# Layer two's first feed-forward: the input projection by seven block products in place of eight

## The reference, cut to what matters

```python
def ada_norm(x, g, shift, scale):
    return rms_norm(x, g) * (1.0 + scale) + shift
def swiglu(h, w_in, w_out):
    a, b = jnp.split(h @ w_in, 2, axis=-1)
    return (jax.nn.silu(a) * b) @ w_out
...
x = x + 0.5 * mx[:, 2] * swiglu(ada_norm(x, norm_g[l, 0], mx[:, 0], mx[:, 1]), ffn_w_in[l, 0], ffn_w_out[l, 0])
hctx = hctx + 0.5 * mc[2] * swiglu(ada_norm(hctx, norm_g[l, 0], mc[0], mc[1]), ffn_w_in[l, 0], ffn_w_out[l, 0])
```

## Time and profile before

| | |
|---|---|
| Median of 3 runs | 2319.11 us (2318.86 to 2327.45) |
| Profiled execution, first to last instruction (span) | 2314.2 us |
| The profiled execution's own time | not listed apart from its span; the two are compared in the prediction |
| Mean granted TensorE clock | 0.987 of full speed |
| TensorE (matmul) | busy 2227.1 us, 96% of the span, 19320 matmuls |
| VectorE | 1145.4 us, 49% |
| ScalarE | 846.8 us, 37% |
| GpSimd | 176.3 us, 8% |
| DMA | 315.76 MB, 136 GB/s on the mean |

### The profile page before, as it was taken

How to read it: one execution, slowest core, us unless ns; L and a number is a source line. 1 busy time by engine, 2 the same in 40 slices (tenths; PEclk the granted TensorE clock), 3 DMA queues, 4 the chain that set the end, 5 groups by cost and what they waited for, 6 DMA issues and landing times. The chain is left out here.

```text
span 2314.2 us, 46991 instructions
## 1 busy us (share of the span) xinstructions
PE 2227.1 (96%) x19320; PEld 2091.2 (90%) x19320; DVE 1145.4 (49%) x1930; ACT 846.8 (37%) x1384; POOL 176.3 (8%) x150
## 2 busy tenths in 40 slices
PE   6999999899999999998999999999999999999998
PEld 5986798799999999976999999999999998979998
DVE  5227375653433445456653333454343446487665
ACT  4226454632221233248432222243232234455444
POOL 0003112100000010501200000010000010001000
PEclk9999999999999999999999999999999999999999
DMA  9853544445676244520354666242233233225573
GB/s 297 234 167 86 172 133 104 128 147 154 186 216 186 86 131 117 149 80 28 102 175 141 190 207 189 84 126 85 81 114 94 86 96 101 74 82 146 168 202 112
DMA packets 515900, 315.76 MB, mean 136 GB/s; under 512 B 16035, under 2 KB 513274, under 8 KB 515622
## 3 DMA queue, kind: packets, MB, share of 16 engines
q1 hardware_dynamic: 515160, 313.45, 46.1%
q10 hardware_dynamic: 590, 0.16, 0.0%
HBM read 312.50 MB, written 1.06 MB: 135 GB/s over the span
## 5 line engine op out<-in xcount | busy, mean ns | idle before, releaser
L1118 PE MATMUL ps<-h_hi,w_hi 128*128 128x256 f32 x3376 | 728.0, 280 | 3.5 <-DVE h_lo L1726 1.7
L1118 PE MATMUL ps<-h_lo,w_hi 128*128 128x256 f32 x3376 | 720.6, 278 | 0.0
L1118 PE MATMUL ps<-h_hi,w_lo 128*128 128x256 f32 x3376 | 720.6, 278 | 0.0
L1118 PEld LDWEIGHTS ps<-h_hi,w_hi 128*128 128x128 f32 x3376 | 537.8, 189 | 22.9 <-issue 21.6
L1118 PEld LDWEIGHTS ps<-h_lo,w_hi 128*128 128x128 f32 x3376 | 539.4, 189 | 0.1
L1118 PEld LDWEIGHTS ps<-h_hi,w_lo 128*128 128x128 f32 x3376 | 537.9, 189 | 0.0
L1960 DVE TENSOR_TENSOR w_lo<-stage,w_hi 128x1024 fp32r<-128x1024 f32 x227 | 285.0, 1258 | 441.5 <-ACT w_hi L1467 440.9
L1467 ACT ACTIVATE w_hi<-stage 128x1024 fp32r<-128x1024 f32 x227 | 236.6, 1055 | 334.4 <-PE ps L1118 200.4
L1960 DVE TENSOR_TENSOR w_lo<-deep,w_hi 128x1024 fp32r<-128x1024 f32 x184 | 226.1, 1234 | 226.9 <-ACT w_hi L1467 225.2
L1467 ACT ACTIVATE w_hi<-deep 128x1024 fp32r<-128x1024 f32 x184 | 191.9, 1055 | 179.7 <-PE ps L1118 141.4
L1118 PE MATMUL ps<-g_hi,w_hi 128*128 128x256 f32 x1100 | 232.9, 280 | 0.2
(11 more groups left out here) (413 smaller groups left out, 2858.0 us busy)
## 6 DMA issues: line engine op xcount, KB each, us to landing
modw<-in_ada_w SPq DMA_DIRECT2D x72, 1024.0 KB, 6.7
stage<-in_ffn_w_in SPq DMA_DIRECT2D x88, 512.0 KB, 3.9
deep<-in_ffn_w_in SPq DMA_DIRECT2D x88, 512.0 KB, 3.9
modw<-in_w_mod SPq DMA_DIRECT2D x18, 1024.0 KB, 6.1
stage<-in_w_in SPq DMA_DIRECT2D x30, 512.0 KB, 5.3
stage<-in_ffn_w_out SPq DMA_DIRECT2D x32, 384.0 KB, 3.5
stage<-in_even_w_in SPq DMA_DIRECT2D x24, 512.0 KB, 4.0
deep<-in_ffn_w_out SPq DMA_DIRECT2D x32, 384.0 KB, 3.4
```

The source lines that it names most:

```text
L1118: last = mm(ps[:, j, v - a:v - a + SEQ], w_part[wp][:, u % RING, c, :], x_part[xp][:, x, v:v + SEQ], start=first and wp == xp and v == a, ...
```

## The change

The product of tokens and a pair of units is seen as a product of 2x2 blocks. The tokens are cut into quarters: 256 latent or context tokens by the first or last 4 chunks of 128 input rows. The weights of a pair are cut likewise: gate unit or up unit by the first or last 4 chunks. Eight block products (of 12 matmuls of 128x256 each) become seven, with sums of blocks as operands, and sums of the results.

- *Weight halves.* Of each pair, seven halves of 128x512 are split into high and low parts: B11 and B21 (the gate unit's), B22 (the up unit's second), and four sums T1 = B12 − B11, T3 = B22 − B12, T2 = T3 + B11, T4 = B21 − T2. GpSimd forms the sums (`pool_seven`), two of them in place over the fetched unit, T1 and T4 in buffers of their own (`t1_raw`, `t4_raw`). ScalarE makes the high part of each half (`act_half`), VectorE the low one (`dve_half`). The ring of 4 units becomes a ring of 8 halves.
- *Token sums.* The seam leaves the tokens in `h_hi` and `h_lo`. GpSimd adds the two for four quarters (`x_quarter`, 128x1024 each) and forms two of the four sums, VectorE the other two; each of the four is split by ScalarE and VectorE.
- *Products.* TensorE goes through the seven in the order of `seven_order`, the next pair's B11, B21, B22, T2 and T1 woven with T3 and T4 of the one before. B11, T3, T4 and T2 add up in one bank (X1, two in turn), the others go to Y1, W1 and Z1.
- *Results.* ScalarE copies three of the results out of PSUM (128x256: `keep_p1`, `keep_z`, `keep_u3`), VectorE adds (`c11`, `u2`, `c12`, `c22`, with one operand in PSUM), ScalarE applies silu to latent and context gate apart (`gate`), GpSimd multiplies gate and up (`gated`, 128x512), ScalarE and VectorE make the high and low part (`high`, `low`).
- *Where.* The second half does all 11 pairs so; the first half does one pair as before (`conv=1`) and 8 in the new way. The seam runs 2 units ahead instead of 3 (`lead=2`). The first half's down projection no longer splits the first units of the next phase; its last block makes the high and low parts of B11 and B21 instead (`opens`). SP fetches a gate unit into its slot only after T4 and T2 of the pair that had it.
- Some tiles (`cst`, `convt`, `wgate`, parts of `vtok`, `big`, `stage`) lend their space, and new counters share semaphores with counters of the mixers (`SHARED`).

```diff
+def seven_order(w):
+
+    order = [("B11", 0)]
+    for p in range(-1, w):
+        here = [("T3", p)] + [("B21", p + 1), ("B22", p + 1)] + [("T4", p)] + [("T2", p + 1), ("T1", p + 1)] + [("B11", p + 2)]
+        order += [(kind, n) for kind, n in here if 0 <= n < w]
+    return order
...
+        def seam(tail, start, norm, dst=None, segs=0, latent=False, lead=LEAD):
+        def seven(w, col0, n, dst, conv=0, sums=False, turn=0):
+
+            units = 2 * (conv + n)
+            r = {"unit_done": units, "w_hi": units + LEAD - 2 * conv, "w_ready": units + LEAD - 2 * conv, "prod": 6 * n, "e_hi": 5 * n, "e_ready": 5 * n,
+                 "t_sum": 4 * n, "c11_sum": n, "u2_sum": n, "c22_sum": n, "c12_sum": n, "p1_kept": n, "z_kept": n, "u3_kept": n, "a_lat": n, "a_ctx": n, "gt_ready": n,
+                 "g_hi_ready": conv + n, "g_ready": conv + n, "bank_free0": conv, "bank_free1": conv}
+            if sums:
+                r.update({"f_full": 4, "s_sum": 2, "s_diff": 2, "sum_hi": 4, "sum_ready": 4})
+            add("seven", r, w=w, col0=col0, n=n, dst=dst, conv=conv, sums=sums, turn=turn, order=seven_order(n))
...
+                if fast:
+                    seven(w, (0, FH)[half] * P + (2 - 2 * half) * P, (FH - 3, FH)[half], (3, 0)[half], conv=1 - half, sums=half == 0, turn=2 * half)
...
+                         fed=not (last and i and half) and not (fast and not half), peel=i and half, opens=fast and not half, hper=hpers[2 * half + 1], **w_down)
...
+            seam(tail, ("ffn_w_in_2", 1, 0), (1, 0), lead=2)
...
+        def half_slot(p, kind, n):
+
+            return (place(p, kind, n) + 2 * (first_unit(p) + p.kw["turn"])) % (2 * RING)
...
+        def raw_half(p, kind, n):
+
+            b, a = (arrival(first_unit(p) + 2 * n + i)[0] for i in range(2))
+            return {"B11": a[:, 0:4, :], "B21": a[:, 4:8, :], "B22": b[:, 4:8, :], "T2": a[:, 0:4, :], "T3": b[:, 0:4, :],
+                    "T1": t1_raw[:, :, :], "T4": t4_raw[:, :, :]}[kind]
...
+            for n in range(k["n"]):
+                col = k["col0"] + (k["conv"] + n) * P
+                eng.wait_ge(S("w_ready"), u0 + 2 * n - DEEP + 1)
+                fetch(u0 + 2 * n, col + D_FF)
+                if n < 2:
+                    eng.wait_ge(S("w_ready"), u0 + 2 * n + 1 - DEEP + 1)
+                else:
+                    eng.wait_ge(S("t_sum"), p.at("t_sum", 4 * (n - 2) + 4))
+                    eng.wait_ge(*half_signal(p, "lo", "T2", n - 2))
+                fetch(u0 + 2 * n + 1, col)
...
+            def product(kind, n, bank, tokens, first):
+                eng.wait_ge(*half_signal(p, "lo", kind, n))
+                at = half_slot(p, kind, n)
+                for c in range(KC // 2):
+                    for wp, xp in W_X:
+                        last = mm(ps[:, bank, 0:SEQ], half[wp][:, at, c, :], tokens(xp, c), start=first and c == 0 and wp == xp,
+                                  stop=c == KC // 2 - 1 and wp == "lo", skip_group_check=True)
+                up(last, "unit_done", by=2) if kind == "T4" else up(last, "prod")
...
+            p1(0)
+            for n in range(-1, w):
+                here, ahead = X1[n % 2], X1[(n + 1) % 2]
+                if n >= 0:
+                    eng.wait_ge(S("u2_sum"), p.at("u2_sum", n + 1))
+                    summed(n, 4)
+                    product("T3", n, here, sum_of(3), False)
+                if n + 1 < w:
+                    eng.wait_ge(S("c11_sum"), p.at("c11_sum", n + 1))
+                    product("B21", n + 1, W1, tokens_of(1, 0), True)
+                    eng.wait_ge(S("z_kept"), p.at("z_kept", n + 1))
+                    summed(n + 1, 2)
+                    product("B22", n + 1, Z1, sum_of(4), True)
+                if n >= 0:
+                    eng.wait_ge(S("u3_kept"), p.at("u3_kept", n + 1))
+                    product("T4", n, here, tokens_of(1, 1), False)
+                if n + 1 < w:
+                    eng.wait_ge(S("p1_kept"), p.at("p1_kept", n + 2))
+                    product("T2", n + 1, ahead, sum_of(2), False)
+                    summed(n + 1, 3)
+                    eng.wait_ge(S("c22_sum"), p.at("c22_sum", n + 1))
+                    eng.wait_ge(S("c12_sum"), p.at("c12_sum", n + 1))
+                    product("T1", n + 1, Y1, sum_of(1), True)
+                if n + 2 < w:
+                    p1(n + 2)
...
+            for n in range(-1, w):
+                act_half(eng, p, "T1", n + 1)
+                if n == w - 1:
+                    act_after_halves(eng, p, 0)
+                if n + 1 < w:
+                    keep_p1(n + 1)
+                if n >= 1:
+                    high(n - 1)
+                if n >= 0:
+                    keep_u3(n)
+                act_half(eng, p, "B11", n + 2)
+                act_half(eng, p, "T3", n + 1)
+                if n + 1 < w:
+                    gate(n + 1, 0)
+                    keep_z(n + 1)
+                act_half(eng, p, "B21", n + 2)
+                act_half(eng, p, "B22", n + 2)
+                if n >= 0:
+                    gate(n, 1)
+                act_half(eng, p, "T4", n + 1)
+                act_half(eng, p, "T2", n + 2)
+            act_after_halves(eng, p, 1)
+            high(w - 1)
+            act_after_halves(eng, p, 2)
 
...
+                    if k.get("opens") and i * step + j == k["n"] - 1:
+                        dve_half(eng, phases[phases.index(p) + 1], "B11", 0)
+                        dve_half(eng, phases[phases.index(p) + 1], "B21", 0)
...
+            if k["sums"]:
+                eng.wait_ge(S("f_full"), p.at("f_full", 3))
+                up(V.tensor_tensor(x_sum[2], x_quarter[2], x_quarter[0], ALU.subtract), "s_diff")
+                dve_half(eng, p, "B11", 0)
+                dve_half(eng, p, "B21", 0)
+                eng.wait_ge(S("f_full"), p.at("f_full", 4))
+                eng.wait_ge(S("s_sum"), p.at("s_sum", 2))
+                up(V.tensor_tensor(x_sum[3], x_quarter[3], x_sum[1], ALU.subtract), "s_diff")
...
+            for n in range(-1, w):
+                dve_half(eng, p, "T1", n + 1)
+                if n >= 0:
+                    c12(n)
+                    c22(n)
+                dve_half(eng, p, "B11", n + 2)
+                if n == w - 1:
+                    dve_split(eng, u0 + 2 * w)
+                if n >= 1:
+                    low(n - 1)
+                if n + 1 < w:
+                    c11(n + 1)
+                for kind, ahead in (("T3", 1), ("B21", 2), ("B22", 2)):
+                    dve_half(eng, p, kind, n + ahead)
+                if n + 1 < w:
+                    u2(n + 1)
+                dve_half(eng, p, "T4", n + 1)
+                dve_half(eng, p, "T2", n + 2)
+            dve_split(eng, u0 + 2 * w + 1)
+            low(w - 1)
+            dve_split(eng, u0 + 2 * w + 2)
...
+            def sums(n):
+                (b, full_b, arrived_b, _), (a, full_a, arrived_a, _) = (arrival(u0 + 2 * n + i) for i in range(2))
+                eng.wait_ge(full_b, arrived_b)
+                eng.wait_ge(full_a, arrived_a)
+                if n:
+                    eng.wait_ge(*half_signal(p, "lo", "T1", n - 1))
+                up(G.tensor_tensor(t1_raw[:, :, :], b[:, 0:4, :], a[:, 0:4, :], ALU.subtract), "t_sum")
+                eng.wait_ge(S("t_sum"), p.at("t_sum", 4 * n + 1))
+                up(G.tensor_tensor(b[:, 0:4, :], b[:, 4:8, :], b[:, 0:4, :], ALU.subtract), "t_sum")
+                eng.wait_ge(S("t_sum"), p.at("t_sum", 4 * n + 2))
+                eng.wait_ge(*half_signal(p, "lo", "B11", n))
+                up(G.tensor_tensor(a[:, 0:4, :], b[:, 0:4, :], a[:, 0:4, :], ALU.add), "t_sum")
+
+            def last_sum(n):
+                a = arrival(u0 + 2 * n + 1)[0]
+                eng.wait_ge(S("t_sum"), p.at("t_sum", 4 * n + 3))
+                if n:
+                    eng.wait_ge(*half_signal(p, "lo", "T4", n - 1))
+                up(G.tensor_tensor(t4_raw[:, :, :], a[:, 4:8, :], a[:, 0:4, :], ALU.subtract), "t_sum")
+
+            def gated(n):
+                for name in ("a_lat", "a_ctx", "c12_sum", "c22_sum"):
+                    eng.wait_ge(S(name), p.at(name, n + 1))
+                eng.wait_ge(S("g_ready"), p.at("g_ready", k["conv"] + n))
+                up(G.tensor_tensor(gt[:, :], gate_of[n % 2], plain, ALU.mult), "gt_ready")
+
+            if k["sums"]:
+                eng.wait_ge(S("w_ready"), p.at("unit_done") - 4)
+                for chunks, v, i, ready in ((0, 0, 2, 4), (1, 0, 3, 8), (0, 1, 0, 12), (1, 1, 1, 16)):
+                    eng.wait_ge(S("h_ready"), p.at("h_ready", ready - 2 * KC))
+                    up(G.tensor_tensor(x_quarter[i], quarter(h_hi, chunks, v).bitcast(F32), quarter(h_lo, chunks, v).bitcast(F32), ALU.add), "f_full")
+                eng.wait_ge(S("f_full"), p.at("f_full", 4))
+                up(G.tensor_tensor(x_sum[0], x_quarter[0], x_quarter[1], ALU.add), "s_sum")
+                eng.wait_ge(S("s_sum"), p.at("s_sum", 1))
```

(37 more changed lines are left out.)

211 lines of the change are left out of this document (192 added, 19 removed).

## The result

The changed kernel takes 2323.61 us (median of 20 runs), the kernel before beside it 2318.99, a difference of 4.6 us between the medians. The ratio estimated from all the runs is 1.0024, 95% interval 1.0013 to 1.0034, or 5.6 us slower (3.0 to 7.9). The forecast was 2321, within 0.5%. 228 matmuls fewer (19 × 12) bought nothing. The profiled execution has a span of 2319.7 us, 5.5 above that of before.

What follows compares the result with a forecast made beforehand. VectorE and GpSimd alternating, 10.65 us a pair, would bound it: −4.4 (pairs) + 2.0 (seam) + 5.0 (start) − 0.9 (second half) + 0.3 (step), so +2 on the 2314.2 span, plus 4.9 around it: 2321 us, range 2303 to 2335.

Steps and rivals of the forecast that it cites:

- The turns: Steady pairs: VectorE and GpSimd exclude each other except for 0.14 us of each instruction, summing to 10.2 us a pair.
- Rival 1: Both halves: TensorE stays the bound, 2295 us, chance 0.11; a partial form 2309 us, chance 0.17.
- rival 2: Steady pairs: whole VectorE and GpSimd instructions exclude each other, 12.0 us a pair, 2346 us, chance 0.09.
- The pair at 10.65: Steady pair: 10.2 us of alternating VectorE and GpSimd work plus 0.45 of gaps, 0.23 less than before.
- The halfway form of rival 2: Steady pairs: exclusion partway to whole instructions, 11.1 us a pair, 2329 us, chance 0.2.
- the steady part of −4.4: Nineteen changed pairs of both halves, each 0.23 us shorter: 4.4 us less.
- The wait ahead of B11: Steady pairs: TensorE waits 1.1 us before B11, since the context gate freeing its bank stands behind ScalarE's copies.
- The seam: Seam before the first half: GpSimd's token quarters delay VectorE's low parts, 2.0 us late, bounds 0 and 6.7.
- The start: First half's first changed pairs: late products cost 5.0 us over the steady loss, bounds 1 and 10.
- Rival 3: First half's start: pauses of 1 to 3 us let the clock fall, +9, 2330 us, chance 0.08.
- The second half: It starts filled, so the engines' alternation falls behind only after three pairs: 0.9 us less.
- The step: Down projections: matmul step may become 0.1179 in the first (+2.4), 0.1133 in the second (−1.8); even odds, +0.3.

Runs made afterwards that it cites:

- the best version: Changed kernel with weight sums, fourth token quarter, quarter sums, gated products on VectorE, gate unit fetched first, new start order, later bank wait: 2301.31 us, ratio 0.9945.
- the run with all four late: Changed kernel with all four GpSimd token quarters held until the unchanged pair's weights have low parts: seam start to down projection 139.3 us, against 133.9.
- the new order at the start: Changed kernel with VectorE's and ScalarE's work reordered in the first half's start: unchanged pair's start to down projection 102.2 us, against 103.0.
- the four edits: Changed kernel with weight sums on VectorE, gate unit fetched first, reordered start, and bank wait behind the first product: ratio 0.9951 to the kernel before.

## Why the prediction was right, and where it was not

**The turns**, which decided it, were right: ends 0.55 and 1.15 us apart, additions from PSUM outside, as the earlier trace rows had it. Rival 1 falls with that, and so does rival 2: whole instructions would have made 12.0 a pair, and the fronts of 0.14 do overlap. The Trainium skill's page SBUF — State Buffer (Who interferes with whom) says that a VectorE instruction with two inputs in SBUF contends with a GpSimd instruction that reads SBUF, and that one with at most one such input, outside the two-port modes, does not. The trace agrees: low parts of 0.69 us take 1.45 to 1.80 beside a GpSimd instruction, and the addition with an operand in PSUM stays at 0.41. That the first holds the other up for its whole instruction the page says of the two-port modes; of these instructions the trace shows less, 0.55 of 0.69 and 1.15 of 1.29.

**The pair at 10.65** was right for the turns and wrong for the kernel, which took 11.14. The step that failed is the one on SP: "its SP waits move from whole splits to the T4 sums and low T2, more than 4 us ahead of need". The gate unit's waits do end early, but SP stands at the up unit's wait for low T3 until then, since that one is ahead in its queue. Both are issued late and land 5.8 us later. With that order turned the pair is 10.65. The halfway form of rival 2 had the size, 11.1, and the wrong cause, and the sign that the prediction gave, "A pair above 11 is rival 2", would have misled: the ends and the turned fetch decide. The steady pairs are 11.1 on the mean, so the term per pair should have been +0.22, not −0.23: the steady part of −4.4 came out near +4.

**The wait ahead of B11**, forecast 1.1, was 0.9 to 1.3. It was forecast with a TensorE of 9.52 a pair; its products took 9.84, since four of the seven step at 0.118 to 0.120. The slower step cost nothing here, because TensorE waits anyway, and 0.3 to 0.4 us a pair in the best version.

**The seam**, forecast 2.0 within 0 to 6.7, took 4.6. The mechanism was right and mis-sized: all but 0.25 of it is the quarters' turns (the run with all four late), half of it among the low parts of the unchanged pair's weights, which the working put into "end about 1584" and not into the seam.

**The start**, forecast 5.0: the four waits of the first pair (B22, T2, T1, T3) were forecast as 1.0, 1.5, 1.1 and 3.3 us and came out as 0.2, 1.4, 0.9 and 3.0. Against steady pairs of 11.1 the first half is 3.2 us longer, the clock's fall included. Rival 3's fall of the clock came once behind a pause of 3.0 us, beside the main case and not in its place.

**The second half**: −1.6 in place of −3.4. Eleven pairs at the steady 11.1 would have taken 2.2 more than before. The first two steps from B11 to B11 that hold a whole pair took 9.87 and 10.38 us, filled ahead, and the beginning and the end, 168 matmuls or two pairs' work, 20.8. Against 11.1 a pair, and with 0.4 in the other pairs, that gave nearly 4 us where 0.9 was forecast. Its entry, priced at nothing, cost 1.3: TensorE waited for all four banks of the down projection ahead of a product that writes a fifth.

**The step** of the first down projection did change (0.1133 to 0.118, +2.3), that of the second did not; the stretch near the end of the program moved by 6.2 the other way. That pauses set the step, as the sum has it, no run shows: in the trace of before, at 2021.7 us, it goes from 0.1178 to 0.1133 among matmuls at most 0.121 apart, and in the changed projections it goes, in the main, with the tile that the tokens come from.

**The median over the span.** Of the 4.9 us that the prediction took for what lies around the span, 1.8 do (the changed kernel's profiled execution has a time of 2321.46 us and a span of 2319.7). The rest is how far the profiled execution of before, some 2316.0 us by that, stood under the median of its runs.

So the total was near for mixed reasons. The steady pair (8.6 us), the seam (2.6) and the entry (1.3) were priced too low, the start (1.8) and the fill of the second half (2.9) too high, which leaves some 8 us; and stretches that the change does not touch gave 3.8 back. Why the runs agree with the span's 5.5, and not with the 9.2 of the changed parts, was not settled: whether the step elsewhere is faster in most runs of the changed kernel, one profile can't show. The reason for "no gain" was right; that the total came so near was partly luck.

## What to carry to other kernels

Before work goes to an idle engine, look in the trace for a stretch where that engine and its neighbours both worked, and compare ends there, not lengths: here 228 matmuls were paid for with GpSimd turns of 1.15 us that VectorE could have done in 0.60. In a queue that issues transfers, the one whose buffer is free first should stand first (here 10.65 us a pair in place of 11.14). A bound that has moved off an engine leaves the earlier waits around it (banks, order, fetch) priced at nothing only until it moves back.

## What the runs showed that was not expected

A matmul of 128x256 steps by 0.1133 us with tokens from one tile and 0.118 to 0.120 from another, in the same bank, stretch and clock. A pause of TensorE ahead of the unchanged pair, 2.46 to 2.48 us from start to start each time, left the granted clock at 1.00 in the changed kernel and let it fall in three of its variants, where the pair then took 1.5 to 1.65 us more; what makes the difference was not found. The windows of the unchanged pair in the changed kernel, with the gate unit fetched first, and with the new order at the start (the third variant is that of the four edits, shown above):

```profile
1583.19:1594.20 11.01, 11.01 (x97) 11.01 (x97) 10.77 (x12) 1.96 (x3) 7.04 (x4) 1.00 0.33 97
1585.74:1598.40 12.66, 12.66 (x97) 12.66 (x97) 12.42 (x14) 3.62 (x4) 7.02 (x4) 0.87 0.30 84
1580.49:1593.09 12.60, 12.60 (x96) 12.60 (x97) 12.36 (x14) 3.57 (x5) 7.03 (x4) 0.86 0.29 85
```

Two VectorE instructions in a row end 0.60 apart, 0.05 more than one behind a GpSimd instruction.
